# Two weight splits swapped, GpSimd's state-space products cut into chunks, and three small reorderings, in a two-layer hybrid block

## The reference, cut to what matters

```python
for l in range(DEPTH):                                   # DEPTH = 2
    h = h + 0.5 * rmsnorm(swiglu(rmsnorm(h), w_gate, w_up, w_down))        # ffn1, inner width 2816
    u = rmsnorm(h) @ w_in                                # split to MLA, NSA, FoX, S5
    y = [mla(u), nsa(u), fox(u), s5(u)]                  # 3 kinds of attention, 1 state space
    h = h + rmsnorm(group_rmsnorm(y) @ w_out)
    h = h + rmsnorm(cross_attention(rmsnorm(h), rmsnorm(mem)))
    h = h + 0.5 * rmsnorm(swiglu(rmsnorm(h), w_gate, w_up, w_down))        # ffn2
```

## Time and profile before

| | us |
|---|---|
| median of three executions | 1301.69 |
| the profiled execution | 1298.99 |
| its span from first to last instruction | 1297.2 |
| TensorE (PE) busy | 1264.6 (97%) |
| VectorE busy | 826.0 (64%) |
| ScalarE busy | 661.7 (51%) |
| GpSimd busy | 239.0 (18%) |
| share of TensorE on the chain that ended last | 92% |

### The profile page before, as it was taken

One profiled execution on the slowest core, in us unless ns is written; L12 is line 12 of the kernel. 1 busy time (PEld: TensorE's weight loads), 2 busy tenths in 40 slices (PEclk: granted clock), 3 DMA queues, 4 the chain that ended last, 5 costly groups with the idle time before them and its releaser, 6 DMA issues.

```text
span 1297.2 us, 18597 instructions
## 1 busy us (share of the span) xinstructions
PE 1264.6 (97%) x6836; PEld 1074.4 (83%) x6836; DVE 826.0 (64%) x1169; ACT 661.7 (51%) x1099; POOL 239.0 (18%) x251
## 2 busy tenths in 40 slices
PE   8999999999899999999999999999998999999998
PEld 6888788899788888888888878888997898888886
DVE  5658858775547575555576588677756465755554
ACT  6454347574436564444564544565645455644442
POOL 1728901000002010000054297000000020100000
PEclk9999999999989999999999999999998999999999
DMA  9654554424414356555455555534245143655551
GB/s 344 259 194 162 189 183 144 150 106 187 170 58 179 130 210 214 185 180 186 166 194 180 188 194 194 186 123 162 86 175 195 62 154 130 234 186 181 179 190 65
DMA packets 32442, 222.36 MB, mean 171 GB/s; under 512 B 3584, under 2 KB 4096, under 8 KB 6784
## 3 DMA queue, kind: packets, MB, share of 16 engines
q1 hardware_dynamic: 30080, 209.28, 45.2%
q10 hardware_dynamic: 2304, 12.29, 2.5%
HBM read 219.46 MB, written 2.10 MB: 171 GB/s over the span
## 4 chain that ended last, share of the span: by engine, by line
PE 92%; DVE 4%; issue 2%; ACT 1%; DMA 0%; POOL 0%; SPq 0%; ACTq 0%; DVEq 0%; POOLq 0%
PE PS L1667 87%; DVE w_lo L1142 2%; PE PS L1784 1%; PE PS L2002 1%; DVE x_lo L1145 1%; ACT w_hi L672 1%; PE PS L1810 1%; DMA raw<-in_weights 0%; DVE work L1145 0%; DVE h L1145 0%; PE PS L2053 0%; DVE mix_out L1142 0%; PE PS L2255 0%; PE PS L2046 0%; PE PS L1986 0%
## 5 line engine op out<-in xcount | busy, mean ns | idle before, releaser
L1142 DVE TENSOR_TENSOR w_lo<-raw,w_hi 128x1024 fp32r<-128x1024 f32 (+1 forms) x378 | 487.6, 1332 | 228.1 <-ACT w_hi L672 224.4
L672 ACT ACTIVATE w_hi<-raw 128x1024 fp32r<-128x1024 f32 x368 | 369.0, 1054 | 239.9 <-PE PS L1667 238.2
L1667 PE MATMUL PS<-w_hi,x_hi 128*128 128x512 f32 (+2 forms) x1104 | 425.6, 385 | 10.1 <-DVE w_lo L1142 5.5
L1667 PE MATMUL PS<-w_lo,x_hi 128*128 128x512 f32 (+2 forms) x1104 | 413.4, 374 | 0.0
L1667 PE MATMUL PS<-w_hi,x_lo 128*128 128x512 f32 (+2 forms) x1104 | 407.6, 375 | 0.0
L1667 PEld LDWEIGHTS PS<-w_hi,x_hi 128*128 128x128 f32 x1104 | 208.2, 189 | 53.8 <-issue 6.5
L1667 PEld LDWEIGHTS PS<-w_hi,x_lo 128*128 128x128 f32 x1104 | 208.1, 189 | 38.2
L1667 PEld LDWEIGHTS PS<-w_lo,x_hi 128*128 128x128 f32 x1104 | 208.6, 189 | 34.5 <-issue 0.5
L522 POOL TENSOR_SCALAR st<-st 128x1 f32<-128x1 f32 x32 | 20.9, 653 | 617.3 <-ACT proj L695 550.8
L1667 PE MATMUL PS<-w_hi,hid_hi 128*128 128x512 f32 x336 | 132.6, 395 | 0.0
L1667 PE MATMUL PS<-w_lo,hid_hi 128*128 128x512 f32 x336 | 131.6, 392 | 0.0
(11 more groups left out here) (277 smaller groups left out, 1335.0 us busy)
## 6 DMA issues: line engine op xcount, KB each, us to landing
raw<-in_weights SPq DMA_DIRECT2D x194, 1024.0 KB, 4.7
pmat<-in_mats ACTq DMA_DIRECT2D x3, 1568.0 KB, 7.7
gain<-in_post ACTq DMA_DIRECT2D x8, 512.0 KB, 3.7
zone<-mem_scratch ACTq DMA_DIRECT2D x2, 1024.0 KB, 5.5
raw<-in_weights SPq DMA_DIRECT2D x3, 512.0 KB, 7.5
h<-in_x SPq DMA_DIRECT2D x2, 512.0 KB, 6.2
zone<-in_mem SPq DMA_DIRECT2D x1, 1024.0 KB, 10.9
mem_scratch<-zone ACTq DMA_DIRECT2D x1, 1024.0 KB, 6.1
```

Of the source, the lines that this page charges most:

```text
L672: a.activation(w_hi[s][:, c_], raw[s][:, c_], ACT.Copy).then_inc(sem[hi_done[s]], 1)
L1142: return v.tensor_tensor(o, x_, y_, op)
L1667: return t_.matmul(o, a_, b_, start=first, stop=last)
```

## The change

Six edits, all of them of order or of place; the same numbers are computed.

1. `split_mid(21)` and `split_mid(22)` trade places on ScalarE and on VectorE.
2. GpSimd's products of the S5 matrices are held at four points: the last three `s_c` products until `hid_t` 7, the small B products until `hid_t` 8, the first three `s_w` products until `hid_t` 9 and the last three until `hid_t` 10.
3. The two 128x1024 copies on GpSimd go: the B products are written to `zone` at their own width (`s_b`), and the matmuls that used the copies read them there. The wait for `mem_scratch` moves ahead with them.
4. At the border from the first feed-forward part to the mixers (`p == 1`) the fills of k = 6 and 7 of the first row tile stand ahead of the first half of h's update of the second row tile.
5. In the first step of each feed-forward part, the last two transposes of the second row tile come after one group of three matmuls instead of two, with a wait for the two fills whose banks they overwrite.
6. At the kernel's start SyncE issues the loads of units 2 and 3 ahead of the memory rows, and unit 4 behind them.

```diff
--- before.py
+++ after.py
@@ -203,7 +203,7 @@
         s_w = [v3(qk_a[:, i * 1024:(i + 1) * 1024], "p (g j c) -> p g j c", g=PAIRS, j=CH) for i in range(2)]
         s_lb = v3(zone[:, 0:2048], "p (i g n) -> p i g n", i=2, g=PAIRS)
 
-        s_b4 = [v3(zone[:, i * 1024:(i + 1) * 1024], "p (g n) -> p g n", g=PAIRS) for i in range(2)]
+        s_b = [v3(zone[:, i * 256:(i + 1) * 256], "p (g n) -> p g n", g=PAIRS) for i in range(2)]
         s_t0 = v3(zone[:, 2048:3072], "p (g r c) -> p g r c", g=PAIRS, r=CH)
         s_cs = [v3(zone[:, 3072 + i * 512:3584 + i * 512], "p (g q) -> p g q", g=PAIRS) for i in range(2)]
         s_c = [v3(zone[:, 4096 + i * 1280:5376 + i * 1280], "p (g j c) -> p g j c", g=PAIRS, j=CH + 1)
@@ -313,7 +313,7 @@
         for name, n in FIRST_PIECES.items():
             CREDIT[name] = CREDIT.get(name, 0) + n
         own = {e: ctx.enter_context(nc.semaphore(f"{e}_order")) for e in ("act", "dve", "pool")}
-        own_steps = {"act": 1, "dve": 66, "pool": 92}
+        own_steps = {"act": 1, "dve": 66, "pool": 90}
         pool_held = ctx.enter_context(nc.semaphore("pool_held"))
         s_con = ctx.enter_context(nc.semaphore("con_in"))
         s_con0 = ctx.enter_context(nc.semaphore("con_first_in"))
@@ -440,11 +440,14 @@
                         sp.dma_start(raw[1][:, half:], weights[1][:, half:]).then_inc(sem[raw_in[1]], 16)
                         sp.dma_start(h3[:, 1], x[P:2 * P, :]).then_inc(x_in[1], 16)
                         sp.dma_start(con[:, 2 * P:], consts[:, 2 * P:]).then_inc(s_con, 16)
+                        load(room(*ffn_unit(l, f, "a", 1)), base + 2)
+                        load(room(*ffn_unit(l, f, "b", 1)), base + 3)
                         sp.dma_start(mem3, memory.rearrange("(t p) d -> p t d", p=P)).then_inc(s_mem, 16)
+                        load(room(*ffn_unit(l, f, "down", 0)), base + 4)
                     else:
                         load(room(*ffn_unit(l, f, "first")), base)
                         load(room(*ffn_unit(l, f, "second")), base + 1)
-                    with sp.Fori(1, FU) as i:
+                    with sp.Fori(2 if l == 0 and f == 0 else 1, FU) as i:
                         load(room(*ffn_unit(l, f, "a", i)), base + i * 3 - 1)
                         load(room(*ffn_unit(l, f, "b", i)), base + i * 3)
                         load(room(*ffn_unit(l, f, "down", i - 1)), base + i * 3 + 1)
@@ -597,6 +600,8 @@
                 tt(s_c[0], crw, over_c(arj, J5, 0), ALU.mult)
                 tt(tc5, ciw, over_c(aij, J5, 0), ALU.mult)
                 tt(s_c[0], s_c[0], tc5, ALU.subtract)
+                pool.wait_ge(*E.at("hid_t", 7))
+                pool.sem_inc(pool_held)
                 tt(s_c[1], crw, over_c(naij, J5, 0), ALU.mult)
                 tt(tc5, ciw, over_c(narj, J5, 0), ALU.mult)
                 g.tensor_tensor(s_c[1], s_c[1], tc5, ALU.add).then_inc(sem["s5_c_done"], 1)
@@ -605,24 +610,28 @@
                     v3(nsa_q[:, 256:512], "p (g c) -> p g c", g=PAIRS)
                 tb3 = v3(nsa_q[:, 512:768], "p (g c) -> p g c", g=PAIRS)
                 krw, kiw = bc(krd, 2, C2), bc(kid, 2, C2)
+                pool.wait_ge(*E.at("hid_t", 8))
+                pool.sem_inc(pool_held)
                 tt(tb1, br, krw, ALU.mult)
                 tt(tb2, bi, kiw, ALU.mult)
-                tt(tb1, tb1, tb2, ALU.subtract)
+                pool.wait_ge(s_memst, 16)
+                pool.sem_inc(pool_held)
+                tt(s_b[0], tb1, tb2, ALU.subtract)
                 tt(tb2, bi, krw, ALU.mult)
                 tt(tb3, br, kiw, ALU.mult)
-                tt(tb2, tb2, tb3, ALU.add)
-                brw, biw = bc(tb1, 2, CH), bc(tb2, 2, CH)
+                tt(s_b[1], tb2, tb3, ALU.add)
+                brw, biw = bc(s_b[0], 2, CH), bc(s_b[1], 2, CH)
+                pool.wait_ge(*E.at("hid_t", 9))
+                pool.sem_inc(pool_held)
                 tw = v3(proj[:, 1280:2304], "p (g j c) -> p g j c", g=PAIRS, j=CH)
                 tt(s_w[0], brw, over_c(arj, CH, 0), ALU.mult)
                 tt(tw, biw, over_c(aij, CH, 0), ALU.mult)
                 tt(s_w[0], s_w[0], tw, ALU.subtract)
+                pool.wait_ge(*E.at("hid_t", 10))
+                pool.sem_inc(pool_held)
                 tt(s_w[1], brw, over_c(aij, CH, 0), ALU.mult)
                 tt(tw, biw, over_c(arj, CH, 0), ALU.mult)
                 tt(s_w[1], s_w[1], tw, ALU.add)
-                pool.wait_ge(s_memst, 16)
-                for q, src in enumerate((brw, biw)):
-                    ts(v3(zone[:, q * 1024:(q + 1) * 1024], "p (g j c) -> p g j c", g=PAIRS, j=CH), src, 1.0, ALU.mult)
-
                 ts(v3(rope_t[:, 0:NCH], "p (g q) -> p g q", g=1), v3(q01, "p (g q) -> p g q", g=1), 1.0, ALU.mult)
                 tt(s_mag, bc(r4, 2, NCH), bc(rope_t[:, 0:NCH], 1, PAIRS), ALU.mult)
                 pool.memset(s_x[0][:, :, 0:1], 0.0)
@@ -1038,12 +1047,12 @@
                 act.wait_ge(*E.at("s5_out", 1))
                 for k in range(2):
                     a.activation(s5_tiles[0][:, k], s_out[:, k], ACT.Copy).then_inc(sem["x_hi_done"], 1)
-                split_mid(21)
+                split_mid(22)
                 act.wait_ge(*E.at("phi_x", 1))
                 a.activation(v3(hx2, "p (a n) -> p a n", n=NC_CMP), v3(hx2, "p (a n) -> p a n", n=NC_CMP),
                                  ACT.Tanh, scale=GELU_S).then_inc(sem["phi_th"], 1)
                 evac_kv(7)
-                split_mid(22)
+                split_mid(21)
                 act.wait_ge(*E.at("phi_out", 1))
                 a.activation(kct[0:HD, 0:NC_CMP], bank(5)[0:HD, 0:NC_CMP], ACT.Copy, scale=0.5)
                 a.activation(vct[0:NC_CMP], bank(5)[0:NC_CMP, 64:128], ACT.Copy, scale=0.5).then_inc(sem["phi_c"], 1)
@@ -1226,8 +1235,11 @@
                     y_gain(q, weight, 1, 0)
                     fill_lo_of(at, p, 0, range(3, 6))
                     E.step(y_gain(q, weight, 1, 1))
+                    if p == 1:
+                        fill_lo_of(at, p, 0, range(6, KT))
                     h_update(q, 1, 0)
-                    fill_lo_of(at, p, 0, range(6, KT))
+                    if p != 1:
+                        fill_lo_of(at, p, 0, range(6, KT))
                     h_update(q, 1, 1)
                     dve.wait_ge(*E.at("h_done", 3 * q + 3))
 
@@ -1761,7 +1773,7 @@
                     if not by_piece:
                         pe.wait_ge(*E.at(split_done[s], ns + 1))
                     for k in range(KT // 2):
-                        if between and k == KT // 4:
+                        if between and k == (2, 1)[t]:
                             between()
                         if by_piece and half == 0:
                             pe.wait_ge(*E.at(split_done[s], k - 2))
@@ -1824,7 +1836,11 @@
 
                     gate_up_tile(f, b_, 1, 0, fill, next_rows).then_inc(sem["gu_half"], 1)
                     pe.wait_ge(*E.at("hid_done", 2 * f * FU))
-                    gate_up_tile(f, a_, 0, 1, fill, lambda: rows_of(p, 1, range(6, KT))).then_inc(sem[unit_done[a_[0]]], 1)
+                    def last_rows():
+                        pe.wait_ge(*E.at("x_split", FILL[fill] + KT + 2))
+                        rows_of(p, 1, range(6, KT))
+
+                    gate_up_tile(f, a_, 0, 1, fill, last_rows).then_inc(sem[unit_done[a_[0]]], 1)
                     gate_up_tile(f, b_, 1, 1, fill).then_inc(sem[unit_done[b_[0]]], 1)
 
                 def ffn_down(f, i, first, last):
@@ -1918,7 +1934,7 @@
                 for i_ in range(2):
                     for q in range(2):
                         for g in range(4 * i_, 4 * i_ + 4):
-                            i = mm(k_ps[g % 4 * C2:(g % 4 + 1) * C2, i_], s_b4[q][:, g, 0:C2], s_c[q][:, g, 0:CH], q == 0, q == 1)
+                            i = mm(k_ps[g % 4 * C2:(g % 4 + 1) * C2, i_], s_b[q][:, g], s_c[q][:, g, 0:CH], q == 0, q == 1)
                 i.then_inc(sem["s5_k"], 1)
                 s, _, _ = mid(l, 0)
                 first_rows_half(1, range(KT)).then_inc(sem[unit_done[s]], 1)
```

## The result

| | before | after |
|---|---|---|
| median of the runs | 1301.28 us (1298.71 to 1302.28, 4 runs) | 1281.07 us (1280.58 to 1282.83, 4 runs) |
| profiled execution, span | 1298.99 us, 1297.2 us | 1280.59 us, 1278.7 us |

The ratio of the times is 0.985, with a 95% interval of 0.9833 to 0.9868: faster by 20 us. The forecast of 1279.7 was the median of 1301.69 less 22.0 us; the profiled execution came down by 18.4. The difference of 3.6 us is what most of this text is about.

What follows compares the result with a forecast made beforehand. TensorE bounds the kernel, with idle time and low clock at scores(2) the main loss; 8.5 + 8.9 + 3.1 + 0.9 + 0.65 = 22.05, so 22.0 us off 1301.69 gives 1279.7 us, range 1276 to 1288 eight times in ten.

Steps and rivals of the forecast that it cites:

- What bounds the kernel: TensorE, busy 1264.6 of 1297.2 us; only its 32.6 us of idle time and its slow running can be won.
- edit 1, the wait: Ahead of scores(2): idle time falls from 4.91 to 0.66 us, 4.25 us won per layer, 8.5 in both.
- Edit 1, the clock: Behind scores(2): no fall to 1.2 GHz, 3.8 us won in the first layer, 5.1 in the second, together 8.9.
- windows at 0.50: Sign around scores(2): if windows at half clock remain, the forecast is wrong; 1.00 was expected in all.
- rival 1: At scores(2): the clock falls all the same, taking back 8.9 us: 1288.6 us; chance 0.08.
- Edit 1, what is late next: At out_rows(1, 0): mixer_lo's fills ready at 360.9, needed at 361.4; margin 0.5 us, no loss taken.
- a wait of ScalarE for a DMA: Sign at ScalarE's split ahead of attention_out(1): a wait for a DMA there shows the forecast wrong.
- Rival 4: Unit 22's load comes late: each us beyond 4.8 costs 1 us per layer; at 15 us, 1309; chance 0.03.
- Edits 2 and 3: GpSimd beside VectorE's splits: loop stall gone, 3.9 us, less 0.8 for late splits: 3.1, between 1.7 and 3.9.
- The step that failed: End of GpSimd's held work: 1.4 us ahead of the first square; a split held up costs 0.4 us per layer.
- Edit 4: Border to the mixers: TensorE's 0.61 us wait for k = 6 goes; 0.45 us per layer, 0.9 in both.
- Edits 5 and 6: First gate, early in the first layer: TensorE's 0.7 us wait goes; 0.65 us, bounds 0 and 0.7.

Runs made afterwards that it cites:

- Experiment 1: Kernel before with only split_mid(21) and split_mid(22) swapped on ScalarE and VectorE: 1283.71 us against 1299.40, ratio 0.9878.
- Experiment 2: Kernel before with ten idle matmuls on TensorE ahead of the wait of scores(2), the wait itself kept: 1291.23 us, ratio 0.993.
- experiment 10: Changed kernel timed again: 1280.65 us, ratio 0.9849; and the even-groups GpSimd kernel plus one idle matmul ahead of the wait of scores(2): 1277.22 us, ratio 0.9818.
- Experiment 6: Changed kernel with attention_out(1) ahead of split_mid(22) on VectorE: 1282.82 us, ratio 0.9877.
- Experiment 3: Kernel before with only GpSimd's products held in groups and its two copies gone: 1297.24 us, ratio 0.9989.
- experiment 4: Changed kernel with each of GpSimd's four held groups released one step earlier (hid_t 6 to 9): 1277.77 us, ratio 0.9828.
- experiment 5: Changed kernel with GpSimd's groups cut evenly, nothing large left for the last step: 1275.56 us, ratio 0.9819.
- experiment 8: Changed kernel with h's update again ahead of the fill of k = 6 and 7 at the border: 1281.00 us, ratio 0.9866.
- experiment 9: Changed kernel with the early transposes and the load order both taken back: 1283.48 us, ratio 0.9876; with only the load order taken back: 1281.36 us, ratio 0.9862.
- experiment 7: Changed kernel with even GpSimd groups, attention_out(1) ahead of split_mid(22) and mixer_lo(1) ahead of attention_max(2) on VectorE: 1276.00 us, ratio 0.9816.

## Why the prediction was right, and where it was off

The 3.6 us between 22.05 and 18.4 are made up so: 2.3 are edits 2 and 3, 1.0 the clock, 0.3 edit 4, 0.1 edits 5 and 6; the wait gave 0.2 more than forecast.

**What bounds the kernel; edit 1, the wait: right.** VectorE's start was given as 347.98; less the 1.2 us by which this trace is ahead there, that is 346.8, and it was 346.72. 0.66 us of idle time were forecast, 0.57 were left. Experiment 1 shows that the swap alone does it.

**Edit 1, the clock: right in kind, off in size.** 8.9 us forecast, 7.9 measured. Experiment 2 shows the mechanism; experiments 1 and 2 put the term without an episode at 4.1 and 5.4 us, 9.5 in all. So the term was put 0.6 too low, and the episode at 991 us, which the sum didn't have, cost 1.6. By its own list the prediction counted windows at 0.50 as a sign that it is wrong (rival 1), and there are such windows. But rival 1 was put as all or nothing, and a third thing happened: short episodes at 1.2 GHz remain, of 3.4 us, in some layers. The rule cited for it (the Trainium skill, "TensorE: Matmul & The Clock Gate", "A second HAM failure mode: psum-queue depth-cycling") names short idle times between groups of matmuls. The traces agree that the clock goes down and up in a stage with such groups, but not that the idle time is needed: experiment 10 took away all but 0.14 us of it and the episode came. Nor did the trace before show the low clock "only after the 4.91 us": it stood at 0.50 from 10.0 to 13.4 us too, at the kernel's start, as in four other executions.

**Edit 1, what is late next: the place right, the margin too wide.** `mixer_lo` started at 358.73, and TensorE came to it at 359.75 without a wait. Experiment 6 pulled TensorE ahead by 0.57 us and got a wait of 0.71 there: of the forecast's margin of 0.5 us next to nothing was real. That it cost nothing was close to luck.

**A sign that was badly chosen.** The prediction said that a wait of ScalarE for a DMA ahead of that split would show it wrong. There is one, 1.26 us, and it is in the forecast's own numbers (ScalarE starts when the load lands). Rival 4 should have been tied to TensorE's wait.

**Edits 2 and 3: the gain right, the loss wrong.** The loop's stall went wholly, 1.97 us per layer as worked out. The step that failed reads: "Held until the tenth transposes end (185.5), it ends at 197.5", and "beside the two splits of 195.80". The start was right: GpSimd begins at 183.24, 0.2 us behind the tenth transposes (182.46 and 0.60 long). But the work took 11.1 us to the last memset and not 12.0, because the 9.1 us for three products came from rows that VectorE's splits had themselves stretched; they took 7.4. And the border's splits came 1.6 us later than without the new wait; so GpSimd was done at 194.3, ahead of them (194.9), and they took 4.64 us as before. The split that it did meet, of the last unit, wasn't in the prediction's list. It stands ahead of the gate, and TensorE had 1 us to spare there before (gate done at 192.6, transposes at 193.59); the split became 2.4 us longer. So the term was 1.58 us per layer instead of 0.4, and edits 2 and 3 gave 0.8 us in all instead of 3.1, less than the 1.7 that the prediction had as their least. Experiment 3 shows it with these edits alone, experiments 4 and 5 take it away by the timing of the groups alone.

**Edit 4: the step was right, the size too large.** "I take 0.45 per layer" was 0.28, by both experiment 8 and the offsets; the second row tile's transposes give back more than was counted. **Edits 5 and 6** gave 0.5 of 0.65 in this pair of traces; the wait that they aim at is gone, the size isn't shown (experiment 9).

The median came nearer (1281.07 to 1279.7) than the sum deserved, and that is luck: the forecast carried over that before, the median lay 2.7 us over the profiled execution; after, it lay 0.5 over. In the three later groups the median of the kernel before was 1298.97 to 1300.48.

## What to carry to other kernels

When work is moved to another time on an engine that slows a neighbour, list every instruction of the neighbour in the new stretch and the spare time behind each, and take the moved work's duration from rows where it ran alone. Here the loop's last step had the least spare time, 1 us, and the kernels with nothing large in it (experiments 5, 7 and 10) were the fastest. Look behind every long wait of TensorE at the windows of the clock: here 4.9 us of waiting cost 9 to 10 us, and idle matmuls alone won back half.

## What the runs showed of the hardware

**The clock falls without a wait.** In several executions it stood at 1.2 GHz for 6.8 us early in the middle part, in a stretch without any idle time of TensorE. Of the kernel of experiment 3, just ahead and then in it; and of the kernel with edits 5 and 6 taken back, in the second layer:

```profile
286.00:292.00 6.00, 6.00 (x55) 6.00 (x54) 3.98 (x10) 4.07 (x5) 0.00 (x0) 1.00 0.31 87
292.00:299.00 7.00, 7.00 (x36) 7.00 (x36) 3.45 (x7) 2.43 (x6) 0.72 (x1) 0.53 0.19 77
```

```profile
922.00:929.00 7.00, 7.00 (x35) 7.00 (x35) 3.24 (x6) 2.17 (x6) 0.72 (x1) 0.51 0.14 57
```

It costs 3.1 us by the offsets. Of the 28 layers in the 14 profiled executions it was in five, and a shorter one of 3.4 us in a sixth. Experiment 3's kernel took 1297.0 to 1297.8 us in seven runs, at a mean granted clock of 0.990 to 0.991, and 1300.9 to 1302.9 in four, at 0.984 to 0.987; the profiled one, with two such episodes, is of these. Behind `scores(2)` an episode of 3.4 us was in 9 of the 24 layers with at most 0.71 us of idle time there, while all four layers with 4.91 us had one of 10 to 14 us. What starts the short ones wasn't found. Going by the mean clocks of the runs they may make up most of the spread of these times, and they are why differences under 2 us were read from offsets in the trace and not from times.

**GpSimd is slowed too, but by less than VectorE.** A product of 128x1024 elements took 1.93 us alone and 2.69 beside a split, the subtraction 2.43 alone (experiment 5) and 3.17 beside a split (the third of the changed kernel's last group): 0.75 us more each time. The split in the last step became 2.4 us longer, and its end, at 191.69, is 1.07 us behind the end of that subtraction, about the length of one of its halves. That agrees with the exclusive lock that the prediction cites from the Trainium skill ("SBUF — State Buffer", "Who interferes with whom").
